# Down projection of a two-block network: 32 of 44 weight tiles multiplied in four blocks of seven products each

## What is computed

```python
D_FF = -(-8 * D_MODEL // (3 * 256)) * 256        # 5632 = 44 x 128
h = rmsnorm_2(x, g_pre_ffn[l]) * (1.0 + sc_f) + sh_f
f = (jax.nn.silu(h @ w_gate[l]) * (h @ w_up[l])) @ w_down[l]
x = x + gt_f * rmsnorm_2(f, g_post_ffn[l])
```

## Time and profile before

| | |
|---|---|
| median of three runs | 3106.01 us |
| the profiled execution's own time | 3104.79 us |
| its span, first to last instruction | 3103.1 us |
| TensorE (PE) busy, of the span | 99% |
| VectorE (DVE) busy | 70% |
| ScalarE (ACT) busy | 37% |
| GpSimd (POOL) busy | 11% |
| down stage, first to last matmul | 2615.2 to 3093.7 us |
| mean DMA rate over the span | 169 GB/s |

### The profile page before, as it was taken

How to read it: one execution, slowest core, us unless ns; L and a number is a source line. 1 busy time by engine, 2 the same in 40 slices (tenths; PEclk the granted TensorE clock), 3 DMA queues, 4 the chain that set the end, 5 groups by cost and what they waited for, 6 DMA issues and landing times.

```text
span 3103.1 us, 41270 instructions
## 1 busy us (share of the span) xinstructions
PE 3061.2 (99%) x15416; PEld 2560.4 (83%) x15416; DVE 2162.6 (70%) x2825; ACT 1156.3 (37%) x1520; POOL 353.6 (11%) x505
## 2 busy tenths in 40 slices
PE   8999999999999999999999899999999999999998
PEld 7888877888878888888888788888888888888887
DVE  6666656868886666777755888888888887555555
ACT  5333343213233333444432354444444444222223
POOL 0111100111100000000000300000000000111113
PEclk9999999999999999999999899999999999999999
DMA  5444454875763444444342356666666665444444
GB/s 189 147 127 130 130 197 157 315 264 220 261 254 143 163 162 150 145 156 155 120 149 95 136 163 177 175 175 175 174 175 174 175 176 176 143 143 136 144 143 168
DMA packets 117980, 523.97 MB, mean 169 GB/s; under 512 B 22048, under 2 KB 22320, under 8 KB 80624
## 3 DMA queue, kind: packets, MB, share of 16 engines
q1 hardware_dynamic: 63920, 321.15, 29.5%
q0 software_dynamic: 50352, 174.40, 19.2%
q10 hardware_dynamic: 3600, 26.98, 2.2%
HBM read 434.13 MB, written 37.76 MB: 152 GB/s over the span
## 4 chain that ended last, share of the span: by engine, by line
PE 97%; DVE 3%; ACT 0%; DMA 0%; issue 0%; DVEq 0%; ACTq 0%
PE PS L1723 18%; PE PS L1304 15%; PE PS L1306 15%; PE PS L1305 15%; PE PS L1726 9%; PE PS L1756 5%; PE PS L1755 5%; PE PS L1754 5%; PE PS L1573 1%; PE PS L1600 1%; PE PS L1357 1%; PE PS L1358 1%; PE PS L1359 1%; PE PS L1588 1%; PE PS L1470 0%; PE PS L1429 0%
## 5 line engine op out<-in xcount | busy, mean ns | idle before, releaser
L1304 PE MATMUL PS<-XHL,WH 128*128 128x512 f32 x1968 | 775.2, 394 | 3.0 <-DVE TMP L2152 1.5
L1306 PE MATMUL PS<-XHL,WL 128*128 128x512 f32 x1968 | 766.1, 389 | 0.0
L1305 PE MATMUL PS<-XHL,WH 128*128 128x512 f32 x1968 | 766.0, 389 | 0.0
L819 ACT ACTIVATE WH<-RAW 128x2048 fp32r<-128x2048 f32 x138 | 263.9, 1912 | 526.1 <-PE PS L1306 518.0
L1304 PEld LDWEIGHTS PS<-XHL,WH 128*128 128x128 f32 x1968 | 369.4, 188 | 91.0 <-issue 10.3
L1306 PEld LDWEIGHTS PS<-XHL,WL 128*128 128x128 f32 x1968 | 369.4, 188 | 77.7
L1305 PEld LDWEIGHTS PS<-XHL,WH 128*128 128x128 f32 x1968 | 369.5, 188 | 77.0 <-issue 2.2
L1766 DVE TENSOR_TENSOR WL<-RAW,WH 128x2048 fp32r<-128x2048 f32 x138 | 316.5, 2293 | 85.4 <-ACT WH L819 85.3
L1156 ACT ACTIVATE QH<-RAW 128x1024 fp32r<-128x1024 f32 x210 | 222.4, 1060 | 254.0 <-PE PS L1726 249.8
L1723 PE MATMUL PS<-XHL,QH 128*128 128x512 f32 x1008 | 316.6, 395 | 0.0
L2607 DVE TENSOR_TENSOR QL<-RAW,QH 128x1024 fp32r<-128x1024 f32 x210 | 256.6, 1223 | 58.5 <-ACT QH L1156 58.4
(11 more groups left out here) (372 smaller groups left out, 4641.2 us busy)
## 6 DMA issues: line engine op xcount, KB each, us to landing
RAW<-w_units_dram SPq DMA_DIRECT2D x268, 1024.0 KB, 4.9
ADA<-w_ada_dram POOLq DMA_DIRECT2D x112, 512.0 KB, 5.5
ADAQ<-w_ada_dram POOLq DMA_DIRECT2D x80, 512.0 KB, 5.5
SUM<-RAW POOLq DMA_DIRECT2D x42, 512.0 KB, 4.5
RAW<-SUM POOLq DMA_DIRECT2D x42, 512.0 KB, 4.5
FR<-f_dram SPq DMA_DIRECT2D x10, 1024.0 KB, 5.5
spill_dram<-SIG POOLq DMA_DIRECT2D x24, 256.0 KB, 2.3
f_dram<-TMP SPq DMA_DIRECT2D x22, 256.0 KB, 6.9
```

Of the source, the lines that this page charges most:

```text
L819: act.activation(WH[:, slot, :], RAW[:, slot, :], ACT.Copy).then_inc(hi_ready, 1)
L1304: pe.matmul(PS[:, bank, :], wh, rh[:, x, :], start=k == 0, stop=False)
L1305: pe.matmul(PS[:, bank, :], wh, rl[:, x, :], start=False, stop=False)
L1306: ins = pe.matmul(PS[:, bank, :], wl, rh[:, x, :], start=False, stop=k == n - 1)
```

## The change

Chunks 1 to 8 of the down stage (32 weight tiles) are taken in four blocks of two chunks each. A block is two "problems" (output columns n and n + 2, for n = 0, 1): the product of a 2 x 2 arrangement of hidden parts (two chunks by two halves of 256 tokens, B11 to B22) with a 2 x 2 arrangement of weight tiles (A11, A21, A22, A12). Each problem is made of seven products (j = 0 to 6) instead of eight. A product is one weight operand (a tile, or a sum of tiles) by one hidden operand (4 tiles x 256 tokens, or a difference), with 2 token groups x 4 tiles x 3 parts = 24 matmuls into two PSUM banks. There are 8 problems and STEPS = 56 products t.

The seven weight operands are A11, sum 3 = A11 + A21, A12, A22, sum 1 = A21 + A22, sum 2 = sum 3 + A22, sum 4 = A12 + sum 2. VectorE makes sum 3 (`block_sum3`); sums 1, 2 and 4 are DMAs of 1 MB that add into their destination in SBUF, issued by GpSimd. The rounded operands lie in a ring of three. The seven hidden operands serve both problems of a block and need four differences on VectorE (`operand_sum`).

Six products are added by VectorE into `RES` or a partial buffer `VP`, two banks at a time (`block_read`); product 5 stays in PSUM banks 0 to 3 across all blocks, and `VP` likewise, and both are added into `RES` in eight instructions (`combined`) during plain tiles 4 to 7. Chunks 0, 9 and 10 stay plain (12 tiles); from the second plain chunk on their rounded weights use the ring of three. The transposes now come at products 0, 2, 4 and 6 of each block, with one load buffer instead of two. GpSimd issues, in order, transposes and sums; SP issues each next tile when its buffer has been read. The diff, cut to the block stage:

```diff
+BLOCKED = 4
+PROBLEMS = 2 * BLOCKED
+STEPS = 7 * PROBLEMS
+PLAIN_CHUNKS = FF_CHUNKS - 2 * BLOCKED
+PLAIN_UNITS = 4 * PLAIN_CHUNKS
+OPERAND_AT = [{8: 0, 9: 1, 10: 2, 12: 3, 13: 4}, {1: 5, 3: 6}]
+FIRST_OPERANDS = {0: 3, 1: 4, 2: 5, 3: 6}
+T_BASE = 4
+READS = {0: 1, 1: 2, 2: 3, 3: 4, 4: 5, 6: 6}
+TURN_AT = {0: 0, 2: 1, 4: 2, 6: 3}
+HIDDEN_AT = {STEPS - 5 + j: j for j in range(4)}
...
+    A11, A21, A22, A12 = (at(n, X0 + off * K, [P, FF_CHUNK * S])
+                          for n, off in (("A11", 32), ("A21", 40), ("A22", 48), ("A12", 56)))
+    WSUM = at("WSUM", T0 + 3040, [P, FF_CHUNK * S])
+    RINGH = [at("RINGH", 48 * K, [P, FF_CHUNK * S], FP32R)[:, :], WH[:, 1, :], WH[:, 0, :]]
+    RINGL = [at("RINGL", 56 * K, [P, FF_CHUNK * S], FP32R)[:, :], WL[:, 1, :], WL[:, 0, :]]
...
+    B11, B12, B21, B22 = f_block(0, 0), f_block(0, 1), f_block(1, 0), f_block(1, 1)
+    F_FROM = [B11, B12, B21, B21, B12, B11, B22]
+    W_FROM = [A11, WSUM, A12, A22, A21, WSUM, A12]
...
+            for q in range(PROBLEMS):
+                s, n = divmod(q, 2)
+                more = q + 1 < PROBLEMS
+                sp.wait_ge(q_lo, Q_BASE + 7 * q + 2)
+                if more:
+                    block_load(q + 1, 0)
+                else:
+                    down_load(4)
+                sp.wait_ge(q_lo, Q_BASE + 7 * q + 5)
+                if more:
+                    block_load(q + 1, 1)
+                else:
+                    down_load(5)
+                sp.wait_ge(q_lo, Q_BASE + 7 * q + 6)
+                if more:
+                    block_load(q + 1, 2)
+                else:
+                    sp.wait_ge(x_ready, X_HID + 2 * FF_CHUNK)
+                    hidden_loaded(2)
+                if n == 0:
+                    sp.wait_ge(t_lo, T_BASE + 7 * (s + 1))
+                    if s + 1 < BLOCKED:
+                        f_load(s + 1)
+                    else:
+                        hidden_loaded(1)
+                if more:
+                    sp.wait_ge(q_lo, Q_BASE + 7 * q + 7)
+                    block_load(q + 1, 3)
...
+            def block_sum1(q):
+                gp.wait_ge(w_sum3, q + 1)
+                gp.wait_ge(a_loaded[2], 16 * (q + 1))
+                gp.dma_start(A21[:, :], A22[:, :], accum_op=ALU.add).then_inc(w_sum1, 16)
+            def block_sum2(q):
+                gp.wait_ge(q_lo, Q_BASE + 7 * q + 2)
+                gp.dma_start(WSUM[:, :], A22[:, :], accum_op=ALU.add).then_inc(later_sums, 16)
+            def block_sum4(q):
+                gp.wait_ge(q_lo, Q_BASE + 7 * q + 3)
+                gp.wait_ge(later_sums, 32 * (FAST + q) + 16)
+                gp.dma_start(A12[:, :], WSUM[:, :], accum_op=ALU.add).then_inc(later_sums, 16)
...
+            for q in range(PROBLEMS):
+                t0, more = 2 * q, q + 1 < PROBLEMS
+                if q % 2 == 0:
+                    turn(t0)
+                block_sum4(q)
+                if q % 2 == 0:
+                    turn(t0 + 1)
+                    turn(t0 + 2)
+                if more:
+                    block_sum1(q + 1)
+                    block_sum2(q + 1)
+                if q % 2 == 0:
+                    turn(t0 + 3)
...
+            def block_hi(t):
+                q, j = divmod(t, 7)
+                if t == 0:
+                    act.wait_ge(q_lo, Q0 + PRODUCTS * FAST)
+                elif t < 3:
+                    act.wait_ge(out_done, O_DOWN + 8 + 4 * t)
+                else:
+                    act.wait_ge(q_done, Q_BASE + t - 2)
+                if j in (0, 2, 3):
+                    act.wait_ge(a_loaded[{0: 0, 2: 3, 3: 2}[j]], 16 * (q + 1))
+                elif j == 1:
+                    act.wait_ge(w_sum3, q + 1)
+                elif j == 4:
+                    act.wait_ge(w_sum1, 16 * (q + 1))
+                else:
+                    act.wait_ge(later_sums, 32 * (FAST + q) + 16 * (j - 4))
+                act.activation(RINGH[t % 3], W_FROM[j][:, :], ACT.Copy).then_inc(q_hi, 1)
...
+            def block_step(t):
+                q, j = divmod(t, 7)
+                s, n = divmod(q, 2)
+                x, y = 4 + 2 * (q % 2), 6 - 2 * (q % 2)
+                bank = (x, y, x, y, x, 2 * n, x)[j]
+                first = j in (0, 1, 4) or (j == 5 and s == 0)
+                pe.wait_ge(q_lo, Q_BASE + t + 1)
+                if n == 0:
+                    pe.wait_ge(t_lo, T_BASE + 7 * s + j + 1)
+                if j in (0, 1):
+                    if q == 0:
+                        pe.wait_ge(out_read, READ0 + O_DOWN + 14 + 2 * j)
+                    else:
+                        pe.wait_ge(w_read, 6 * (q - 1) + (4, 6)[j])
+                elif j != 5:
+                    pe.wait_ge(w_read, 6 * q + READS[j - 2])
+                elif q == 0:
+                    pe.wait_ge(taken, TAKEN0 + 4 * FAST)
+                    pe.wait_ge(copied, COPIED0 + 3 * FAST)
+                wh, wl = RINGH[t % 3], RINGL[t % 3]
+                for i in range(2):
+                    out = PS[:, bank + i, :]
+                    for k in range(FF_CHUNK):
+                        fh, fl = (f[j][:, k, i * P:(i + 1) * P] for f in (FOPH, FOPL))
+                        pe.matmul(out, fh, wh[:, k * S:(k + 1) * S], start=first and k == 0, stop=False,
+                                  skip_group_check=True)
+                        pe.matmul(out, fh, wl[:, k * S:(k + 1) * S], start=False, stop=False, skip_group_check=True)
+                        ins = pe.matmul(out, fl, wh[:, k * S:(k + 1) * S], start=False, stop=k == FF_CHUNK - 1,
+                                        skip_group_check=True)
+                ins.then_inc(q_done, 1)
...
+            def block_lo(t):
+                v.wait_ge(q_hi, PRODUCTS * FAST + t + 1)
+                v.tensor_tensor(RINGL[t % 3], W_FROM[t % 7][:, :], f32(RINGH[t % 3]), ALU.subtract).then_inc(q_lo, 1)
+            def block_sum3(q):
+                for i in range(2):
+                    v.wait_ge(a_loaded[i], 16 * (q + 1))
+                v.tensor_tensor(WSUM[:, :], A11[:, :], A21[:, :], ALU.add).then_inc(w_sum3, 1)
+            def block_read(t):
+                q, j = divmod(t, 7)
+                s, n = divmod(q, 2)
+                if j == 5:
+                    return
+                x, y = 4 + 2 * (q % 2), 6 - 2 * (q % 2)
+                bank = (x, y, x, y, x, None, x)[j]
+                acc = VP[:, n, :, :] if j == 0 else quarter((1, 0, 0, 1, None, 1)[j - 1], (n + 2, n, n + 2, n + 2, None, n)[j - 1])
+                v.wait_ge(q_done, Q_BASE + t + 1)
+                if j == 0 and s == 0:
+                    v.tensor_copy(acc, PS[:, bank:bank + 2, :]).then_inc(w_read, 1)
+                else:
+                    v.tensor_tensor(acc, acc, PS[:, bank:bank + 2, :], ALU.subtract if j == 4 else ALU.add)\
+                     .then_inc(w_read, 1)
...
+            for t in range(STEPS):
+                s, o = divmod(t, 14)
+                v.drain()
+                if t >= 1:
+                    block_read(t - 1)
+                if t + 2 < STEPS:
+                    block_lo(t + 2)
+                else:
+                    down_lo(t + 6 - STEPS)
+                if t in FIRST_OPERANDS:
+                    operand_lo(0, FIRST_OPERANDS[t])
+                elif o in OPERAND_AT[1]:
+                    operand_lo(s, OPERAND_AT[1][o])
+                elif s + 1 < BLOCKED:
+                    if o in OPERAND_AT[0]:
+                        operand_lo(s + 1, OPERAND_AT[0][o])
+                    if 7 <= o <= 10:
+                        operand_sum(s + 1, o - 6)
+                if t % 7 == 5 and t + 2 < STEPS:
+                    block_sum3(t // 7 + 1)
+                if o in TURN_AT:
+                    turn(4 * s + TURN_AT[o])
+                if t in HIDDEN_AT:
+                    hidden_lo(1, HIDDEN_AT[t])
+            v.drain()
+            block_read(STEPS - 1)
```

More of the change, by code:

```diff
@@ L487, in _ @@
             down_load(1)
[L488 to L498, removed]
+            sp.wait_ge(q_done, Q0 + PRODUCTS * (FAST - 1) + 3)
+            f_load(0)
+            sp.wait_ge(q_done, Q0 + PRODUCTS * FAST)
+            hidden_saved(FF_TILES - 1, f_d[FF_TILES - 1], 1)
+            block_load(0, 0)
+            block_load(0, 1)
+            sp.wait_ge(lo_ready, D_BASE + 1)
+            down_load(2)
+            block_load(0, 2)
+            block_load(0, 3)
+            sp.wait_ge(lo_ready, D_BASE + 2)
+            down_load(3)
+            for q in range(PROBLEMS):
[26 more added lines that the diff above has]
+                    block_load(q + 1, 3)
+            for n in range(6, PLAIN_UNITS):
+                sp.wait_ge(lo_ready, D_BASE + n - 1)
                 down_load(n)
@@ new lines, in turn, with combined @@
+            def turn(t):
+                v.wait_ge(turn_loaded[t % 2], 16 * (t // 2 + 1))
+                if t == 0:
+                    v.wait_ge(f_saved[1], 8 * FF_TILES)
+                else:
+                    v.wait_ge(turn_saved, 64 * t)
```

(15 more changed lines are left out.)

231 lines of the change are left out of this document (172 added, 59 removed).

## The result

The changed kernel takes 3079.3 us, the median of six runs (3076.3 to 3084.0), against 3105.1 us before: ratio 0.9916, 95% interval 0.9904 to 0.9929, faster by 0.8%. Forecast were 3065.5 us and a range of 3061 to 3091. It wins 26 us where the matmuls alone are worth 43.5. The runs lie 7.7 us apart, those of before 2.5.

What follows compares the result with a forecast made beforehand. TensorE was taken to bound the kernel, busy 99% of the span. 3104.8 - 43.5 (matmuls) + 3 (loop of the sums) = 3064.3 us by the profiled execution, 3065.5 by the median; range 3061 to 3091.

Steps and rivals of the forecast that it cites:

- Matmuls, 43.5 us: Blocked tiles of the down stage: 1344 matmuls replace 1536, removing 192 x 0.2267 = 43.5 us.
- VectorE: In the blocks: 66.7 us of work per 76.2 us block, 88%, lag at most 2.9 us, costing nothing.
- Rival 3: In the blocks: VectorE is the bound, two-bank reads take 1.37 us or gaps widen; 3067 to 3075 us, chance 0.09.
- An accumulate of 1 MB, landing in 7.2 us: Sums in the blocks: each holds the DMA engines 5.5 us and lands 7.2 us after issue.
- The loop of the sums: In the blocks: sums and roundings take 30.5 to 37.7 us against 38.1 per problem; 3 us lost over seven passages.
- a spill of 1 or 2 us: In the blocks: two megabytes of hidden tiles in every other problem can add 1 or 2 us to the loop.
- The first and last plain chunks ... Nothing: Plain tiles around the blocks: VectorE needs 10.0 and 9.8 of 10.88 us per tile; TensorE's wait taken as 0.
- rival 2: In the blocks: accumulates dearer still (8.2 us), change slower, 3117 us; chance 0.07 including what reaches no change.
- The 0.88 of the DMA engines: In the blocks: DMA engines busy 67 of 76.2 us per block, near enough to full that order matters.
- rival 1: In the blocks: sums set the pace moderately, accumulates at 6.5 us, 25 us come back; 3073 to 3099, chance 0.21.
- Its sign: In the blocks: VectorE waits for ScalarE's rounding of products 5 and 6, TensorE for reads behind them.
- The rule of the Trainium skill's page: DMA rings: a 1 MB load would hold a sum up for its full 2.7 us, and a load would wait likewise.

Runs made afterwards that it cites:

- x4: Changed kernel with weight tiles 2 and 3 requested earlier at the start, the last hidden tiles requested earlier, and sum 3 made one product earlier: 3063.1 us.
- e4: Changed kernel with sum 4 adding only 64 of 2048 columns: 3067.1 us.
- y3: Changed kernel with the weight tiles of problems 1 to 7 loaded half (columns 0 to 1023): 3067.3 us.
- e1: Changed kernel with SP's six loads at the start reordered, weight tiles 2 and 3 asked for before the block's A11/A21 and A22/A12: 3081.5 us.
- e2: Changed kernel with one SP wait changed: the last hidden tiles are asked for once the ones before have landed, not once VectorE has split them: 3073.6 us.
- y1: Changed kernel with sum 3 made one product earlier, GpSimd's order kept: 3066.8 us.
- x1: Changed kernel with the 16 transposes moved from products 0, 2, 4, 6 to products 7, 9, 11, 13 of a block: 3081.8 us.

## Why the prediction was right, and where it was not

- **Matmuls, 43.5 us: right.** x4's stage takes 435.2 us for 1920 matmuls against 478.5 before, 43.3 less; its median is 42.0 us under before.
- **VectorE: right.** It was named as hidden with a lag of up to 2.9 us. In x4 it is busy 257 us of 305 (0.84; 0.88 was forecast) without a hole in TensorE's work, e4 and y3 too, with the transposes and reads where the change has them. The read of two banks, taken at 1.15 us back to back, lasts 1.221 and its successor starts 1.14 later. Rival 3 falls.
- **An accumulate of 1 MB, landing in 7.2 us: right.** The sum 4 of the first problem took 7.2; 7.9 is the median of sum 1, with loads beside it.
- **The loop of the sums: the right mechanism, 3 us too short.** It was put at 30.5 to 37.7 us and measured at 40.8 in every other problem and 38.1 in the rest. VectorE and ScalarE, 10.6 us in the prediction, took 11.0 (2815.49 to the issue of sum 1 at 2818.08, and 2847.94 to 2856.33). The DMAs, 19.9 alone and at most 27.1, took 29.9: sum 1 and 2 together 17.9 and sum 4 12.0 from issue to landing. The mis-sized term is the company: 7.2 us for two loads and a transpose, where 10.0 were measured. Three weight loads, two transposes and the hidden tiles were asked for beside the loop in that problem. The prediction named the hidden tiles, with a spill of 1 or 2 us in every other problem; sum 4 took 2.9 us longer there than in the second problem, where the DMAs together took 26.7. The blocks lost 7.6 us; 3 were forecast, with 10 as the end.
- **"The first and last plain chunks ... Nothing": wrong**, and the larger error, 11.0 us. The step counted VectorE's work in tile 2 (10.0 of 10.88 us) and looked at what holds a bank. It did not go through SP's queue in that place: five loads with 6 MB were put ahead of or around weight tiles 2 and 3, and one wait ahead of tile 6. e1 and e2 close the two holes by SP's order alone. The holes are 3.3 and 2.7 us of waiting, and the rest is matmuls at the lower clock behind them, which the forecast named only with rival 2.
- **The 0.88 of the DMA engines: 0.85 measured**, and it was not what mattered: the same share runs with and without holes.
- The time came out in the range of rival 1 (3073 to 3099), but with its mechanism giving only 7.6 of 18.5 us, and that by what stood beside the sums and not by the dearer accumulate it assumed. Its sign, VectorE waiting for the rounding of product 6 with TensorE waiting for the reads behind it, did show. So the range held by luck as much as by reason: 11.0 of the 18.5 us came from a place that the prediction had put at nothing.
- The rule of the Trainium skill's page "DMA: Bandwidth & Descriptors", section "Queues, rings and completion order", that an engine goes round its rings and drains a whole packet of one at a time: y3 shows that halved loads shorten the landing of sums by 2.1 and 1.6 us. That agrees with rings that take turns. No run here tells whole packets from smaller pieces.

## What to carry to other kernels

When the engine that should never wait still stalls, and every other engine is below 90%, look for a cycle of waits from one step back to itself, add up its links over a whole period (here two problems), and compare with the time of that period. Shortening it by moving one instruction ahead of others in its queue (here one line, 12.5 us) was worth as much here as halving the weight loads beside it (y3, 12.1 us), and it leaves every engine its work. And where a new stage begins or ends, walk through each DMA queue in order with megabytes and deadlines: what stands ahead of the first old load is new. What was won ahead of the stage bound by the loop was given back in it here (e1, in one trace), so fix the loop first.

## What the runs showed that was not expected

- A hole in TensorE's work is followed by the lower of its two clock levels in some places and not in others. In the change the clock stayed at 1.00 after the wait of 2.18 us at 2854 and was 0.50 for 5 us after one of 2.73 us at 2991; in e1 one of 2.32 us led to 0.66. The length of the wait alone does not tell: 3.08 us in y1 led to nothing, 1.82 us in x1 to eight slow matmuls. A matmul then starts 0.43 us after its neighbour instead of 0.23, and a hole costs up to about twice its length (2.73 us of waiting, 5.9 lost). What decides was not tried.
- Scatter came with the holes: the runs of the change lie 7.7 us apart, those of x4 0.7.
- Two ways to relieve the blocks each nearly closed the hole at the end as well (e4 and y1, 5.9 to 1.0 and 0.8 us), since the end's requests hang on the last problem's sum 4.
